# The last block's expert gathers in two token halves, the first half's second network beside block 2's

## The chip, the cores and the metric

One NeuronCore of a Trainium2 chip runs the whole program. The metric is device time in microseconds (us) of one execution, lower is better. TensorE (PE) multiplies matrices, VectorE (DVE) and ScalarE (ACT) work element by element, GpSimd (POOL) issues the gathers, SyncE (SP) issues the other transfers, and 16 DMA engines carry both.

## The reference, cut to what matters

Two networks run one after the other on 512 tokens of 1024 numbers, in float32.

```python
h = h + token_mix(rmsnorm(h, w), ...)            # attention and a gated recurrence
h = h[:, N_META:]
h = h + peer_ffn(rmsnorm(h, ffn_w), ...)         # expert layer
x = rmsnorm(h, final_norm_w)                     # end of the first network
...
# peer_ffn, per token: 8 heads choose 16 experts each, by the top 16 of two lists of keys
u = u_table[experts]                             # 128 rows of 1024 numbers
hid = gelu(einsum('nkd,nd->nk', u, xb)) * gates
y = einsum('nk,nkd->nd', hid, v_table[experts])
...
# second network
q, k, v, z_a, u_b, v_b, z_b, g_a, g_b = split(rmsnorm_2(x, g) @ w_in)
y_a = stick_breaking_attention(q, k, v) * silu(z_a)   # 8 heads of 64, causal
y_b = spatial_gating(gelu(u_b), gelu(v_b), ...) * silu(z_b)
merged = sigmoid(g_a) * (y_a @ w_up_a) + sigmoid(g_b) * (y_b @ w_up_b)
x = x + merged @ w_out
return rmsnorm_2(x, final_norm_g)
```

`spatial_gating` mixes the 128 tokens of a chunk through a masked matrix: a token of the first 64 sees only the first 64, so a half of 64 tokens can be computed once it and what stands before it are there.

## The kernel before, in words

**Blocks and gathers.** The 512 tokens are four blocks of 128 (0 to 3). The expert layer of a block takes 128 gathers (`SLOTS`); each fetches 128 rows of 8 KB (u and v of one expert side by side), 1 MB, into one of 8 places of a ring (`RING`). All 512 gathers are one queue of POOL. A gather serves 64 tokens with two experts each; even gathers serve the first 64 tokens of the block and odd ones the second 64. Two gathers make one **tick**, so the program has 256 ticks, 64 to a block. In a tick DVE forms the dot products with u (L2046), ACT applies the gelu, DVE spreads the results into a 128x64 matrix per gather (L2055, L2056), and PE adds the v rows to the block's sums `psum_y` (`weighted_rows`; matmuls named py). Only then is the ring place free for the next gather.

**The rest beside it.** Everything else (the first network of later blocks, the key scores, the second network of earlier blocks) is put between the ticks by `make_plan`, a list `PLAN` that all engines follow in its order. The second network runs for the groups `POST = [(0, 1), (2,), (3,)]`. For each group its weights pass by once, as 60 tiles of 512 KB (SP, L816): 28 for q, k, v and the gates (`q2 k2 v2 za ub vb zb`), 16 for `ga gb`, 8 for `ua ud`, 8 for `wo`. There are 4 places for tiles (`NW`); at the end 7 more in the ring (`XW`). Group (0, 1) stands in ticks 128 to 206 and group (2,) ticks 207 to 255.

**The end.** When the last gather's sums are there, block 3 has its whole second network left: `hu` takes the sums, norms and turns them, then 60 tiles follow, with the 8 heads' stick-breaking attention between them (`zp` scores, `zl` logarithms, `zd` on DVE, `ze`, `zt` transposes, `zv` values), and at the end `ya`, `yo`, `ua`, `mh`, `wo`, `fl`. The first load of this stretch waits until the last gather has landed.

**Choosing.** `top_part` finds a head's 16 experts in 6 parts, one per tick, a head each 8 ticks, two heads ahead of the gathers. It is DVE work.

**Banks.** PE writes into three PSUM banks pa (emptied by ACT) and three pb (emptied by DVE), taken in turn, and two for `psum_y`.

Of the kernel before, what the change touches and what calls it, by code (L numbers as in the profile page):

```python
# [21 lines left out]
W = 512  # L22
HA, DH = 4, 64
# [30 lines left out]
POST = [(0, 1), (2,), (3,)]  # L54
# [10 lines left out]

def heads_per_unit(b):
    return max(1, 4 // (b + 1)) if b != 2 else 1
# [8 lines left out]
def units2(g):  # L76
    return [(b, u) for b in g for u in range(H2 // heads_per_unit(b))]
# [132 lines left out]
def second_rows(g):  # L210


    n = 2 // len(g)
    rows = shared(tiles("q2", g) + tiles("k2", g), 7 // n)
    for name in ("v2", "vb", "ub", "zb"):
        rows += pairs_of(tiles(name, g), n)
    for k, b in enumerate(g):
        rows[-3 + k - len(g) + 1].append(("ln", b))
        rows[-2 + k - len(g) + 1].append(("l2", b))
    gate = pairs_of(tiles("za", g), n)  # L220
# [14 lines left out]
    for c in range(2):  # L235
        up = pairs_of(tiles("ga", g, c), n) + [[("ua", g, c, i) for i in range(2)]]
        if len(g) == 1 and c == 0:
            rows[-1] = rows[-1] + up.pop(0)
        rows += up
        rows += pairs_of(tiles("gb", g, c), n) + [[("ud", g, c, i) for i in range(2)]]  # L240
    wo = tiles("wo", g, 0) + tiles("wo", g, 1)
    if g != POST[0]:
        return rows + [[("mt", b) for b in g]] + pairs_of(wo, n)
    b = g[-1] + 1
    rows += [[("mt", k) for k in g] + [("ldnorm",)]]
    wo = shared(wo, 6)
    for i, name in enumerate(("n1", "m1", "n2")):
        wo[2 + i] = wo[2 + i] + [(name, b)]
    return rows + wo + [[("fin", k) for k in g], [("fd", g[0])], [("fd", k) for k in g[1:]] + [("store", k) for k in g] + [("n3", b)]]


def last_rows(b):
# [6 lines left out]
    fill += [[("ud", g, 0, i) for i in range(2)], [("ud", g, 1, 0)], [("ud", g, 1, 1)]]  # L259
    between = {0: ("hx", b), 2: ("ln", b), 3: ("l2", b), 4: ("sg", b), 5: ("yb", b)}  # L260
    n_units = H2
    for n in range(n_units + 3):
        row = {4: [("fin", b - 1)], 5: [("fd", b - 1), ("store", b - 1)]}.get(n, [])
        for lag, names in ((3, ("zv",)), (2, ("zt",)), (1, ("zd", "ze"))):
            if 0 <= n - lag < n_units:
# [3 lines left out]
        if n < n_units:  # L269
            row += [("zp", b, n // 2)] * (n % 2 == 0) + [("zl", b, n)]  # L270
        rows.append(row + fill[n])
# [6 lines left out]
def use(s):  # L278
# [16 lines left out]
    if name in ("ua", "ud"):  # L295
# [5 lines left out]
            "xt": (0, 2, 0), "s1": (1, 0, 1), "n3": (0, 2, 0), "zs": (0, 1, 0), "zp": (0, 2, 0), "zt": (1, 0, 0), "zv": (1, 0, 0),  # L301
            "sg": (0, 1, 0), "yt": (2, 0, 0), "yb": (1, 0, 0), "yo": (1, 0, 0), "mt": (2, 0, 0), "mh": (1, 0, 0),
            "hu": (0, 2, 0), "qt": (1, 0, 0), "kt": (1, 0, 0)}.get(name, (0, 0, 0))
# [95 lines left out]

def make_plan():  # L400
# [13 lines left out]
    spread(second_rows((2,)), 3 * PER_BLOCK + 15, n, ticks)  # L414
    place_keys(ticks)
    out = []
    for k in range(n):
        b = k // PER_BLOCK
        out += [("dots", k), ("gelu", k)]
        if k % PER_BLOCK == 0 and b:  # L420
            out.append(("take", b - 1))
        g = k // PER_HEAD + LEAD
        if g < HEADS and k % PER_HEAD < 6:
            out.append(("tk", g // HP, g % HP, k % PER_HEAD))
        out += [("mix", k), *ticks[k], ("rows", k)]
    return first + out + [("ldlast",)] + flat(last_rows(NB - 1))
# [3 lines left out]
SUMS_AT = {(s[0][0], s[1]): n + 1 for n, s in enumerate(s for s in PLAN if s[0] in ("r1", "a1"))}  # L430
MIXED_AT = {(s[0][0], s[1]): n + 1 for n, s in enumerate(s for s in PLAN if s[0] in ("r2", "a2"))}
# [42 lines left out]


def stick_bank(b, u):

    return B_AT[("zp", b, u // 2)] - 1 + u % 2 if b == NB - 1 else B_AT[("zs", b, u)]
# [40 lines left out]
def build(nc, t, out):  # L519

    ctx = ExitStack()
    with ctx:
# [3 lines left out]
        def sem(name):  # L526
# [16 lines left out]
        sc = cut(sb("sc", 2 * W)[:, :], 2, W)  # L543
        xnT = cut(sb("xnT", KT * P)[:, :], KT, P)
        qp = cut(sb("qp", 4 * P)[:, :], 4, P)
        fw = sb("fw", D)[:, :]
        tk = Arena(sb("tk", 992 + 2 * BATCH * TOK), 0, 992 + 2 * BATCH * TOK)
        small = Arena(sb("small", 1193), 0, 1193)
# [16 lines left out]
        ss = small.take(22)  # L565
        rs = small.take(21)
# [11 lines left out]
        bs = small.take(NG)  # L578
        iota = small.take(TOP)
# [4 lines left out]
        last_ss = small.take(4)  # L584
        last_tot = small.take(2)
        last_ln, last_half, last_r1, last_r1s, last_ln2, last_s, last_s8 = (small.take(1) for _ in range(7))
# [95 lines left out]
        sga = cut(q2_words, GM2, W)  # L682
        sgb = za
# [4 lines left out]
        ub_last, zb_last, vc_last, vq_last, up_last = (p4.take(W) for _ in range(5))  # L688
        ga_last, gb_last = cut(p4.take(2 * W), 2, W), cut(p4.take(2 * W), 2, W)
        yT_last, merged_last = p4.take(KT * P), p4.take(D)  # L690
        q_rows, k_rows = p4.take(W), p4.take(W)
# [31 lines left out]
        half_ready, hw_ready, y1_read = sem("half_ready"), sem("hw_ready"), sem("y1_read")  # L723

# [6 lines left out]
                  ("normg2", normg2), ("ffnwT", ffnwT), ("bs", bs))  # L731
        LOADED_F, LOADED_C = 16 * len(FIRST), 16 * len(CONSTS)
        POST_CONSTS = 4
        SCORES_READ = {("k2", POST[1]): HEADS - HP + 2, ("v2", POST[1]): HEADS - HP + 4,
                       ("k2", POST[2]): HEADS - HP + 6, ("v2", POST[2]): HEADS}
# [10 lines left out]
        def index2(b):  # L746
            return b - POST_OF[b][0]
# [23 lines left out]

        def key_inputs(b):

            return xn2T[:, :, P * (b - 2):P * (b - 1)] if b >= 2 else xnT
# [9 lines left out]
        def gather_y(b):  # L784

            return SLOTS * (b + 1)

        def norm_weights(b, last):
# [3 lines left out]
            if b == NB - 1:  # L792
                return uv_rows[:, (GATHERS - RING) % RING, 0:D], ld_l, 16
# [3 lines left out]
        def _(sp):  # L797
# [50 lines left out]

            def load_residual(b):
                sp.dma_start(h1[:, b, :], t["x"][P * b:P * (b + 1), :]).then_inc(ld_h, 16)  # L850

            for s in PLAN:
# [23 lines left out]
                elif s[0] == "store":  # L876
                    b = s[1]
                    sp.wait_ge(fin_ready, b + 1)
                    sp.dma_start(out[P * b:P * (b + 1), :], h1[:, b, :]).then_inc(stored, 16)
                elif s[0] == "fl":  # L880
                    for c in (1, 0):
                        half = slice(W * c, W * (c + 1))
                        sp.wait_ge(*((fin_ready, NB) if c else (half_ready, 1)))
                        sp.dma_start(out[P * s[1]:P * (s[1] + 1), half], h1[:, s[1], half]).then_inc(stored, 16)
# [6 lines left out]
            sp.wait_ge(stored, 16 * (NB + 1))  # L891

        @block.tensor
        def _(pe):
# [32 lines left out]

            def rows_tile(src, g, i, n_tiles, bank, full, k0=0):
# [5 lines left out]
                for j, ps in enumerate(open_banks):  # L934
                    for k in range(2):
                        last = mm(ps[:, :], src[:, k0 + 2 * i + k, P * j:P * (j + 1)], w[:, k, :],
                                  i + k == 0, i == n_tiles - 1 and k == 1)
# [7 lines left out]
            def halves_tile(src, c, i, halves):  # L945
# [5 lines left out]
                for k in range(2):  # L951
                    last = mm(halves[c][:, :], src[:, 2 * i + k, :], w[:, k, :], i + k == 0, i == 3 and k == 1)
# [4 lines left out]
            def quarter_transposes(src):  # L957

                ps = a_bank()
                for k in range(4):  # L960
                    last = nc.tensor.transpose(ps[:, P * k:P * (k + 1)], src[:, P * k:P * (k + 1)], ident)
                last.then_inc(a_full, 1)
# [171 lines left out]
            def weighted_rows(k):  # L1134
                b = k // PER_BLOCK
                first, final = k % PER_BLOCK == 0, (k + 1) % PER_BLOCK == 0
                if first:
# [3 lines left out]
                    for c in range(2):  # L1141
                        mm(psum_y[c][:, :], ident, h1[:, b, W * c:W * (c + 1)], True, False)
                pe.wait_ge(mix_ready, k + 1)
                for lo in range(0, BATCH, TG):
# [8 lines left out]
            def stick_scores(b, u):  # L1153
                nh, nk = heads_per_unit(b), P * (b + 1)
                g = POST_OF[b]
                q = cut(q2_words[:, 0:4 * P * len(g)], 4, P * len(g))
                if u == 0 and b == g[0]:
                    pe.wait_ge(a_free, A_AT[("k2", g, 3)])
                ps = b_bank()
                for m, hh in enumerate(unit_heads(b, u)):  # L1160
                    r = slice(DH2 * (hh % 2), DH2 * (hh % 2 + 1))
                    mm(ps[:, nk * m:nk * (m + 1)], q[r, hh // 2, P * index2(b):P * (index2(b) + 1)], k2T[r, hh // 2, 0:nk],
                       True, False)
                    last = mm(ps[:, nk * (m + 1) - P:nk * (m + 1)], ident, stri, False, True)
                last.then_inc(b_full, 1)

            def paired_scores(b, pair):
                q = cut(q2_words[:, 0:4 * P], 4, P)
                if pair == 0:
                    pe.wait_ge(a_free, A_AT[("kt", b)])  # L1170
                banks = [b_bank(), b_bank()]
                for part, ps in enumerate(banks):
                    r = slice(DH2 * part, DH2 * (part + 1))
                    mm(ps[:, :], q[r, pair, :], k2T[r, pair, :], True, False)
                for ps in banks:
                    mm(ps[:, W - P:], ident, stri, False, True).then_inc(b_full, 1)
# [1226 lines left out]
```

## Time and profile before

| | |
|---|---|
| median of 3 runs | 1957.14 us (1956.62 to 1957.34) |
| the profiled execution | 1955.42 us, span 1953.6 us |
| PE, DVE, ACT, POOL busy | 84%, 68%, 34%, 31% of the span |
| mean granted TensorE clock | 0.934 |
| transfers | 729 MB, mean 373 GB/s |

The span is the time from the first to the last instruction; the execution's own time is 1.8 us more. A profile row for a matmul counts records: a float32 matmul is two records, so a weight tile used by one block of 128 tokens (2 matmuls of 512 columns) is 4 records.

### The profile page before, as it was taken

What the parts mean: (1) busy time and instruction counts of PE and PEld (TensorE: products, weight loads), DVE (VectorE), ACT (ScalarE), POOL (GpSimd) and SP (SyncE); (2) the same over time, 40 slices, a digit from 0 to 9 for tenths busy, and PEclk for the clock granted to TensorE, in tenths of its full rate; (3) what the DMA queues carried; (4) which work ended last, traced back from release to release, by engine and by line L of the source; (5) the groups of instructions that cost most, each with busy time, mean ns of one, the idle gap of its engine ahead of it and who ended that gap; (6) DMA issues with size and microseconds to landing.
All of it is one profiled execution on the core that took longest, in us unless ns stands there. A gap on an engine that the chain in (4) does not pass through costs nothing.

```text
span 1953.6 us, 19684 instructions
## 1 busy us (share of the span) xinstructions
PE 1634.3 (84%) x6534; PEld 799.7 (41%) x6534; DVE 1328.8 (68%) x3466; ACT 656.3 (34%) x1224; POOL 600.0 (31%) x529
## 2 busy tenths in 40 slices
PE   7987897779889976888589999789986877877998
PEld 7555553235455443244145434333333322322453
DVE  4356877875788797875876577976665569744242
ACT  3222424242343254222231233521221246311472
POOL 1002333432333343334433333343323325422000
PEclk9997998889999998889899999899998988899999
DMA  7559999999999998999999999999999999999863
GB/s 223 179 169 416 417 417 419 408 417 418 386 413 354 355 416 326 380 419 415 422 413 418 418 414 374 362 400 418 419 417 350 418 419 401 421 418 412 326 235 109
DMA packets 128836, 729.03 MB, mean 373 GB/s; under 512 B 14688, under 2 KB 15856, under 8 KB 63200
## 3 DMA queue, kind: packets, MB, share of 16 engines
q0 software_dynamic: 74272, 537.82, 67.5%
q1 hardware_dynamic: 54464, 189.97, 25.5%
q8 instruction: 52, 0.85, 0.2%
q14 instruction: 48, 0.39, 0.1%
HBM read 725.63 MB, written 2.10 MB: 373 GB/s over the span
## 4 chain that ended last, share of the span: by engine, by line
PE 47%; DMA 23%; DVE 18%; ACT 5%; issue 5%; POOL 1%; POOLq 0%; DVEq 0%; SPq 0%; ACTq 0%
PE pa L919 26%; DMA uv_rows<-in_peer_uv,small 14%; PE py L919 13%; DMA wbuf<-in_wt 8%; PE pb L919 7%; DVE uv_rows L2046 6%; ACT area L1371 2%; ACT L1365 2%; POOL uv_rows L2291 1%; DVE tk L2056 1%; DVE area L2144 1%; DVE tk L2055 1%; DVE small L2033 1%; ACT small L1371 1%; DVE small L1951 0%
## 5 line engine op out<-in xcount | busy, mean ns | idle before, releaser
L2291 POOL DMA_INDIRECT uv_rows<-in_peer_uv,small x512 | 592.2, 1157 | 1182.3 <-PE py L919 967.2
L2046 DVE CUSTOM_DVE_ANT_0 uv_rows<-uv_rows,xrep 128x1024 f32<-128x1024 f32 x512 | 615.7, 1223 | 223.5 <-DMA uv_rows<-in_peer_uv,small 220.6
L919 PE MATMUL py<-uv_rows,tk 128*64 128x512 f32 x2048 | 560.8, 674 | 211.8 <-DVE tk L2056 208.1
L919 PE MATMUL pa<-wbuf,area 128*128 128x512 f32 (+2 forms) x784 | 342.0, 587 | 27.4 <-DMA wbuf<-in_wt 26.7
L1371 ACT ACTIVATE small<-small 128x2 f32<-128x2 f32 (+4 forms) x327 | 70.6, 217 | 849.9 <-DVE small L2046 816.2
L919 PEld LDWEIGHTS py<-uv_rows,tk 128*64 128x64 f32 x2048 | 135.7, 148 | 514.6 <-DVE tk L2056 278.3
L1365 ACT ACT_TABLE_LOAD x250 | 320.8, 1283 | 5.4 <-DVE small L2177 1.0
L919 PE MATMUL pa<-area,wbuf 128*128 128x256 f32 (+2 forms) x1280 | 233.7, 341 | 17.5 <-issue 12.0
L919 PEld LDWEIGHTS pa<-area,wbuf 128*128 128x128 f32 x1280 | 201.3, 199 | 70.6 <-issue 44.5
L919 PEld LDWEIGHTS pa<-wbuf,area 128*128 128x128 f32 (+1 forms) x784 | 134.2, 189 | 229.5 <-issue 176.5
L1371 ACT ACTIVATE area<-pa 128x512 f32<-128x512 f32 (+7 forms) x225 | 89.2, 413 | 267.3 <-PE pa L919 238.0
L919 PE MATMUL pb<-wbuf,area 128*128 128x512 f32 x304 | 142.3, 612 | 11.1 <-DMA wbuf<-in_wt 7.3
L2055 DVE TENSOR_TENSOR tk<-small 128x2 f32<-128x2 f32 x256 | 41.7, 163 | 104.5 <-issue 51.7
L919 PEld LDWEIGHTS pb<-wbuf,area 128*128 128x128 f32 x304 | 55.8, 193 | 97.3 <-issue 81.7
L2056 DVE TENSOR_TENSOR tk<-small,tk 128x128 f32<-128x128 f32 x256 | 74.8, 292 | 8.9
L919 PE MATMUL pa<-area 128*128 128x64 f32 (+7 forms) x392 | 67.7, 345 | 13.7 <-ACT area L1371 12.3
L1371 ACT ACTIVATE area<-area 128x512 f32<-128x512 f32 (+3 forms) x104 | 67.6, 657 | 33.1 <-DVE area L1842 22.7
L919 PE MATMUL pb<-area 128*128 128x128 f32 (+7 forms) x434 | 73.9, 321 | 1.6 <-ACT area L1371 0.9
L919 PEld LDWEIGHTS pa<-area 128*128 128x128 f32 (+2 forms) x392 | 51.2, 207 | 45.3 <-issue 35.3
L919 PEld LDWEIGHTS pa<-xnT,wbuf 128*128 128x128 f32 x512 | 60.2, 194 | 20.0 <-issue 16.4
L919 PE MATMUL pa<-xnT,wbuf 128*128 128x128 f32 x512 | 64.6, 282 | 2.0 <-DVE xnT L1800 1.1
L919 PEld LDWEIGHTS pb<-area 128*128 128x128 f32 (+2 forms) x434 | 53.9, 192 | 18.7 <-issue 12.6
(253 smaller groups left out, 1178.0 us busy)
## 6 DMA issues: line engine op xcount, KB each, us to landing
wbuf<-in_wt SPq DMA_DIRECT2D x300, 512.0 KB
uv_rows<-in_wt SPq DMA_DIRECT2D x36, 512.0 KB, 6.6
uv_rows<-in_peer_uv,small POOLq DMA_INDIRECT x512
wbuf<-in_skT SPq DMA_DIRECT2D x11, 256.0 KB
h<-in_x SPq DMA_DIRECT2D x4, 512.0 KB
an<-in_x SPq DMA_DIRECT2D x3, 512.0 KB
out<-h SPq DMA_DIRECT2D x3, 512.0 KB, 8.3
area<-in_finw SPq DMA_DIRECT2D x2, 512.0 KB, 10.1
```

What stands on the lines that cost most here:

```text
L919: return nc.tensor.matmul(o, l, r, start=start, stop=stop, skip_group_check=True)
L1365: nc.scalar.preload_act_table_set(TABLES[func])
L1371: return nc.scalar.activation(dst, src, func, **more)
L2033: V.tensor_scalar(gate[to, cols], gexps[tok, g % 2, s_::TG], gsum[tok, g % 2, 1:2], None, ALU.mult)
L2046: last = V.tensor_tensor_reduce(uv_rows[:, n % RING, 0:D], uv_rows[:, n % RING, 0:D], xrep[:, b % 2, n % TG, :], 1.0, 0.0, ALU.mult, ALU.a ...
L2055: step(V.tensor_tensor(wcol[:, k % 2, :], dots[:, at:at + BATCH], gate[:, col:col + BATCH], ALU.mult))
L2056: V.tensor_tensor(mix_w[k % 2], token_mask.unsqueeze(1).broadcast_to([P, BATCH, TOK]), wcol[:, k % 2, :].unsqueeze(2).broadcast_to([P, BAT ...
L2144: step(V.tensor_tensor_scan(rcs[:, 0:wide][:, ::-1], seg2[:, 0:wide], soft[:, 0:wide][:, ::-1], 0.0, ALU.mult, ALU.add))
L2291: nc.gpsimd.indirect_dma_start(uv_rows[:, n % RING, :], None, t["peer_uv"], bass.IndirectOffsetOnAxis(ap=expert_ids[:, c:c + 1].bitcast(U3 ...
```

## The change

The gathers of block 3 are put in the order of its halves: 64 for its first 64 tokens (ticks 192 to 223), then 64 for the second. The halves are blocks of their own, 4 and 5 in the code (`HALVES`), here called **half a** and **half b**. The second network's groups become (0, 1), (2, half a) and (half b).

Group (2, half a) again has 49 ticks, 207 to 255, but its order is written out row by row in `late_rows`: block 2's own q, k, v tiles in rows 0 to 5, its attention (a head each two rows) from row 6; half a's sums are taken in row 17 (tick 224); its own q, k, v tiles in rows 18 to 23; the 40 tiles of gates and up projections for both from row 24 to 43, two a row; `wo` in rows 45 to 48. So 12 tiles more are loaded, and each shared tile is multiplied for 128 and for 64 tokens. Half a's attention is 4 units of two heads, with scores at rows 24, 26, 28, 30.

A tile for 64 tokens is multiplied by `product`: the 512 columns are cut in two halves of 256, which go to the lower and the upper 64 partitions of one bank. The end (`last_rows`) is the same network for half b, 60 tiles with 4 units of attention between them, two groups of 4 tiles to a unit. Choosing the experts goes to a head in 6 ticks from tick 142 on (`chosen_part`), so that all heads of block 3 are chosen by tick 214. The final norm and store of block 2 and half a stand in the rows of the end.

```diff
-POST = [(0, 1), (2,), (3,)]
+HALVES = (NB, NB + 1)
+POST = [(0, 1), (2, HALVES[0]), (HALVES[1],)]
...
+LATE = 49
+FIRST_HALF = 17
...
+def late_rows(g):
...
+    at = {(b, u): 6 + 2 * u for u in range(n_units(b))}
+    at.update({(h, u): FIRST_HALF + 7 + 2 * u for u in range(n_units(h))})
...
+    for i, pair in enumerate(pairs_of(tiles("q2", (b,)) + tiles("k2", (b,)) + tiles("v2", (b,)))):
+        put(i, *pair)
+    own = tiles("q2r", (h,)) + tiles("k2r", (h,)) + tiles("v2", (h,))
+    both = [s for name in ("vb", "ub", "zb", "za") for s in tiles(name, g)]
+    for gate, up in (("gb", "ud"), ("ga", "ua")):
+        for c in range(2):
+            both += tiles(gate, g, c) + [(up, g, c, i) for i in range(2)]
+    for i, pair in enumerate(pairs_of(own + both)):
+        put(t + i, *pair)
+    for i, pair in enumerate(pairs_of(tiles("wo", g, 0) + tiles("wo", g, 1))):
+        put(t + 27 + i, *pair)
...
+DENSE = PER_HEAD * 17 + 6
+def chosen_part(k):
+    if k < DENSE:
+        return k // PER_HEAD + LEAD, k % PER_HEAD
+    return 17 + LEAD + 1 + (k - DENSE) // 6, (k - DENSE) % 6
...
-    spread(second_rows((2,)), 3 * PER_BLOCK + 15, n, ticks)
+    for k, row in enumerate(late_rows(POST[1])):
+        ticks[n - LATE + k] += row
...
+            def product(ps, b, rows_, w, start, stop):
+
+                if b not in HALVES:
+                    return mm(ps[:, :], rows_, w, start, stop)
+                for q in range(2):
+                    last = mm(ps[side(q), 0:H], rows_, w[:, H * q:H * (q + 1)], start, stop)
+                return last
...
+                    for i in range(BATCH):
+                        n = BATCH * k + i
+                        for c in range(2):
+                            last = mm(psum_y[c][cell(m, c), :], mix_w[k % 2][:, i, :], uv_rows[:, n % RING, D + W * c:D + W * (c + 1)],
+                                      False, final and i == BATCH - 1)
```

## Rows read from the trace of the kernel before

**Rows 1.** The page: busy shares, the transfers in 40 slices, one group.

```profile
PE 1634.3 (84%) x6534; PEld 799.7 (41%) x6534; DVE 1328.8 (68%) x3466; ACT 656.3 (34%) x1224; POOL 600.0 (31%) x529
...
GB/s 223 179 169 416 417 417 419 408 417 418 386 413 354 355 416 326 380 419 415 422 413 418 418 414 374 362 400 418 419 417 350 418 419 401 421 418 412 326 235 109
...
L2056 DVE TENSOR_TENSOR tk<-small,tk 128x128 f32<-128x128 f32 x256 | 74.8, 292 | 8.9
```

**Rows 2.** The chain that ended last, from 1780 us on: start, us, what.

```profile
1786.45 23.00 DMA uv_rows<-in_peer_uv,small
...
1815.75 14.00 PE pa L919 x32
...
1919.68 0.70 DVE uv_rows L2153
...
1947.88 0.70 DVE h L1977
```

**Rows 3.** The timeline of SP and of PE around the last gather.

```profile
1809.52 1.75 SPq L816 DMA_DIRECT2D wbuf<-in_wt  x4
...
1811.52 1.94 PE L919 MATMUL py<-uv_rows,tk 128*64 128x512 f32 x8 [1.89 <-DVE tk L2056]
```

**Rows 4.** Windows: stretch, length; PE, PEld, DVE, ACT, POOL busy; clock, DMA share, GB/s.

```profile
941.10:981.90 40.80, 21.01 (x74) 5.67 (x72) 34.01 (x92) 9.89 (x19) 19.65 (x17) 0.86 1.01 421
1191.80:1244.10 52.30, 43.81 (x163) 19.91 (x161) 43.00 (x107) 28.55 (x45) 20.69 (x18) 0.84 0.92 352
1244.10:1283.90 39.80, 28.46 (x118) 11.18 (x120) 36.63 (x97) 20.44 (x35) 15.31 (x16) 0.87 0.95 367
...
1490.60:1614.30 123.70, 96.11 (x370) 43.46 (x371) 73.74 (x198) 33.96 (x61) 35.55 (x31) 0.91 1.01 412
1614.30:1694.50 80.20, 59.74 (x226) 22.68 (x225) 74.71 (x198) 44.08 (x79) 37.56 (x33) 0.83 1.00 411
1694.50:1809.40 114.90, 93.12 (x262) 30.98 (x260) 49.61 (x99) 16.72 (x29) 31.95 (x28) 0.97 1.00 408
```

**Rows 5.** The same stretches for line L2046 alone: 4 records are one tick.

```profile
941.10:981.90 40.80, 19.56 (x32) 0.86 1.01 421
...
1490.60:1614.30 123.70, 38.50 (x64) 0.91 1.01 412
```

**Rows 6.** The timeline of PE beside group (0, 1)'s tiles: start, us, instruction.

```profile
1065.56 1.94 PE L919 MATMUL py<-uv_rows,tk 128*64 128x512 f32 x8
1067.43 3.70 PE L919 MATMUL pa<-wbuf,area 128*128 128x512 f32 x8
1071.06 1.94 PE L919 MATMUL py<-uv_rows,tk 128*64 128x512 f32 x8
```

**Rows 7.** The timeline of PE in the end, one attention unit between tiles.

```profile
1853.73 0.60 PE L1182 MATMUL pa<-ident,area 128*128 128x128 f32 x4
1854.26 1.13 PE L919 MATMUL pb<-area 64*128 64x512 f32 x4
1855.32 0.71 PE L919 MATMUL pb<-stri,ident 128*128 128x128 f32 x4
1855.87 3.60 PE L919 MATMUL pa<-uv_rows,area 128*128 128x512 f32 x8
1859.30 3.60 PE L919 MATMUL pa<-wbuf,area 128*128 128x512 f32 x8
1862.73 1.00 PE L919 MATMUL pa<-area 128*128 128x64 f32 x8
```

**Rows 8.** Windows in the end and in two stretches of low clock, columns as in rows 4.

```profile
1820.00:1840.00 20.00, 19.11 (x56) 8.78 (x55) 0.03 (x1) 3.07 (x6) 0.00 (x0) 1.00 1.03 410
...
1815.70:1919.60 103.90, 102.91 (x348) 52.82 (x348) 32.06 (x42) 59.18 (x93) 0.00 (x0) 1.00 0.75 279
...
1480.00:1500.00 20.00, 6.53 (x32) 3.49 (x33) 13.62 (x34) 0.58 (x3) 8.06 (x6) 0.73 0.97 377
...
1600.00:1700.00 100.00, 76.53 (x277) 28.41 (x274) 90.97 (x236) 51.40 (x93) 46.35 (x39) 0.82 1.00 412
```

More of the change, by code:

```diff
@@ L578, in build @@
         bs = small.take(NG)
+        bs_half = cut(small.take(2 * (NG // 2)), 2, NG // 2)
         iota = small.take(TOP)
@@ L955, in halves_tile, with transposed_into, quarters @@
                     open_banks.remove(c)
[L957 to L962, printed above, removed]
+            def transposed_into(ps, parts, full):
+                for k, part in enumerate(parts):
+                    last = nc.tensor.transpose(ps[:, P * k:P * (k + 1)], part, ident)
+                last.then_inc(full, 1)
+            def quarters(src):
+                n = src.shape[1] // P
+                return [src[:, P * k:P * (k + 1)] for k in range(n)]
             def first_rows(name, i):
@@ L1593, in _, with take_quarter_columns @@
+            def take_quarter_columns(dst, ps, end=True):
+                for i in range(2):
+                    last = fn(dst[:, i::2, :], cut(ps[:, P * i:P * (i + 1)], 2, TOK), ACT.Copy)
+                if end:
+                    last.then_inc(a_free, 1)
+            weighed, turned_n = 0, 0
             for s in PLAN:
@@ new lines, in half_rows_up @@
+                    V.tensor_tensor(an[r, 0:W], psum_y[c][r, :], weights, ALU.mult).then_inc(u_ready, 1)
+                ps = cut(bank()[:, :], 4, P)
+                for c in range(2):
+                    last = V.tensor_tensor(turned((b,))[:, 4 * c:4 * c + 4, :], ps[:, :, cell(b, c)],
+                                           normg2[:, 4 * c:4 * c + 4].unsqueeze(2).broadcast_to([P, 4, TOK]), ALU.mult)
+                emptied(last)
+                dve.wait_ge(sq_done, m + 1)
+                fold(half_tot[:, m, :], half_ss[:, m, :], ss_ready)
@@ L2084, in last_products, with half_out @@
+            def half_out(b):
+                col = 16 + nth(b)
+                dve.wait_ge(rf_done, nth(b))
+                dve.wait_ge(ld_f, 16)
+                for q in range(2):
+                    last = V.scalar_tensor_tensor(x1(b)[side(q), :, :], x1(b)[side(q), :, :], rs[side(q), col:col + 1],
+                                                  cut(fw[side(q), :], 2, 2, H)[:, :, q, :], ALU.mult, ALU.mult)
+                last.then_inc(fin_ready, 1)
             def last_products(b, c):
-                half = slice(W * c, W * (c + 1))
+                col = 16 + nth(b)
```

767 lines of the change are left out of this document (476 added, 291 removed).

## The prediction

> **What bounds the kernel now.** I read the page first, its 40 slices before its shares. From the fourth slice to the 37th the transfers run mostly at 413 to 422 GB/s [rows 1], with dips; only the last three slices fall to 326, 235 and 109. PE's 84% is an average over these two stages. In the first the ring of gathers and the weight tiles fill the DMA engines, and I take 418 GB/s as their rate: a gather of 1.049 MB costs 2.51 us, a tile of 0.524 MB 1.25 us, so a tick without tiles 5.02 us and one with two tiles 7.53 us.
>
> The chain shows the other stage. Its last long DMA piece ends at 1809.45 us, when the last gather has landed; from 1815.75 on it is PE nearly all the way to 1919.6, then a serial part to 1953.6 [rows 2]. The windows say the same: in 1815.7 to 1919.6 PE is busy 102.9 of 103.9 us while the transfers run at 279 GB/s [rows 8]. So the end is PE's: from the last py, over at 1813.5 [rows 3], it takes 140.1 us.
>
> Before that, in ticks 208 to 255, three windows (2 x 64 records of L2046 are 32 ticks) run at 408 to 412 GB/s [rows 4, 5]: the transfers bind there, about 1.5% short of their rate.
>
> **The end, for half b.** 8 records of 512 columns take 3.43 us (1855.87 to 1859.30, [rows 7]), 0.43 each, so a tile for 128 tokens costs 1.72 us and 60 cost 103 of the 140. For 64 tokens a tile is 8 records of 256 columns, written alternately to the lower and upper 64 partitions. The trace has no such record, but the py matmuls alternate the same way: 8 records of 512 columns, period 1.87 us [rows 6], half of 3.43. Two at a time they overlap. A pair of 256 columns then costs 0.215 and the tile 0.86 us. Bounds: 0.86, or 1.72 if the halves did not overlap; the floor per small record does not bind, since 8 records of 64 columns fit into 1.00 us [rows 7]. I take 0.86, because py is the same form but for its length. 60 tiles are 51.6 us. A unit of half b's attention is 4 score records of 448 columns in pairs and 4 short ones (1.4 us with a switch of shape), 4 transposes (0.8 with two switches), 16 records of values (1.7): 3.9 us, and 4 units 15.6. Spatial gating and the remaining transposes add 5. PE has 72 us of work.
>
> The weights need more: 60 tiles at the 410 GB/s of [rows 8] are 76.8 us, and none can be asked for before the last gather lands (the load is issued at 1809.52, [rows 3]). With 1.9 us for 0.8 MB of results stored meanwhile and 1 us until the stream runs, the last tile is there 79.7 us after that landing. Its product takes 0.9, and what stands behind the last product today 5.7 (1947.88 to the end, [rows 2]): 86.3. The chain must also hold: in the last rows of attention few tiles are left to multiply, and transposes, exponentials, values, `ya`, `yo`, `ua`, `mh` follow each other. By the same prices that serial part ends at about the same time; I add 2.7 for the two getting in each other's way. From the landing 89 us, against 144.1 before. Counted from the last py it is 83: 4 less for the same distance as today, and 2 because PE will be the later one there (below) and some tiles are in by then. **The end: 140.1 to 83, -57.**
>
> **Ticks 207 to 255.** Twelve tiles and 0.26 MB of norm weights more are 15.7 us at 418 GB/s. That much is sure as long as transfers bind. But they may not. From row 24 on each tick holds two tiles for block 2 (2 x 1.72) and for half a (2 x 0.86) and its py (1.71): 6.87 us. To this come switches between 128 and 64 columns. The period of a py and 8 records is 5.50 us (1065.56 to 1071.06, [rows 6]) and the work in it 5.14, so two switches cost 0.36. The row goes block 2, half a, block 2, half a, py: four switches, 0.72. PE needs 7.59 us a tick and the transfers 7.53: even. What comes on top has no cover. In ticks 231 to 244 that is half a's attention (15.6), the last value and transpose steps of block 2 (2.4), spatial gating of both (2 x 16 records, 3.6) and `yb`, `yo` (1.4): 23 us. The tiles of both groups hold two of three pa banks for two ticks, and attention steps beside them must wait for ACT; where PE works alone such waits are not hidden: 0 to 12, I take 5. Of the sum 4 is off, since today's stretch has its own 1.5% of waits. So +24, bounds 8 (most of it absorbed by the lead of ring and tiles) and 45 (each attention step waits some 3 us).
>
> Half a's `hu` (DVE on the sums, four transposes, ACT's squares and seven small ones) stands in tick 224, where no tile is due before and few after; the same step costs 4.2 us at the end now (1811.52 to 1815.75, [rows 2, 3]). A tick there is 5.0 to 7.5 us of transfers and the ring holds four ticks: I cost it at nothing, 4 us if the ring were empty. The `ldhalf` load stands on SP ahead of half a's tiles, eleven ticks without tiles earlier; late, it would hold those. Block 2's attention in ticks 213 to 230 is what stands in ticks 224 to 239 today at 411 GB/s with DVE busy 74.7 of 80.2 us [rows 4], now without the choosing of experts on top.
>
> **Choosing faster.** In ticks 120 to 127 DVE is busy 34.0 us, 19.6 of it dots [rows 4, 5] and at least 2.3 mixing (8 x 0.29 of L2056, [rows 1]), so choosing costs at most 12.1 us per head, 1.5 us a tick; in 6 ticks instead of 8 it is 0.5 more from tick 142 to 214. Mostly that is idle time of DVE. In the two windows of ticks 160 to 175 it is not: DVE busy 43.0 of 52.3 and 36.6 of 39.8 us, transfers down to 352 and 367 GB/s [rows 4]. With 4 us more work each, up to 8 us; I take 6, low end 0 (a ring that catches up), high end 10.
>
> **Sum.** 1953.6 + 15.7 + 24 + 6 - 57 = 1942.3 us of span, and 1.8 outside it: 1944. This stands against the profiled 1955.4; the median of the runs is 1.7 higher, so one can read a gain of 11 to 12 us, 0.6%.
>
> **The rivals.** *Transfers go on binding* (chance 0.22): the 24 us of the mixed ticks shrink to 0 to 4, choosing is absorbed: 1953.6 + 15.7 + 4 - 57 + 1.8 = 1918 to 1924. For it: in the three windows of ticks 208 to 255 the transfers run at 408 to 412 GB/s with PE busy 74% to 81% [rows 4]. Against it: 23 us of PE work with no gap to fall into.
>
> *The mixed ticks cost more* (0.14), the one that ends on the other side: each attention step of half a waits for a bank that ACT has not emptied, and PE stands with a group open. The 25 ticks from 231 are 8.9 us each in my sum. At 9.4 the gain is gone; at 9.8 the time is 1966.
>
> *The clock falls in the end* (0.08). PE will wait about 0.4 us for every tile. Granted clock is 1.00 while PE is full, but 0.73 in a window with 6.5 of 20 us busy and 0.82 in one with 76.5 of 100 [rows 8]. At the lower level, 1.2 GHz, a tile costs 1.72 us, over its 1.28 of transfer, and PE binds again. Half the end there adds 36 us of PE work less the 5 of slack: 1975. Against it: a PE that falls behind is full again, and full stretches show 1.00.
> The Trainium skill, page "TensorE: Matmul & The Clock Gate", section "HAM oscillation — how this bites in real kernels", warns of just this: a kernel that waits for a transfer at every step is put back to the slow clock each time. By that rule throughout, PE's work in the end would be 144 us and the time about 2015.
> The rows do not bear that out as far as they go (1.00 in a window with 19.1 of 20 us busy), and the sum keeps the full clock.
>
> *The halves do not overlap* (0.03): each half tile 1.72 us, the end as long as before and 41 us more in the mixed ticks: over 2030.
>
> The remaining 0.53 is my forecast, its own range 1932 to 1955.
>
> **The numbers.** A measurement tells 0.2%, 3.9 us, from no change. Faster (under 1953.2): nearly all of the first rival and of the forecast less its upper edge, 0.71. Same: that edge and the near part of the second, 0.11. Slower 0.18. The range 1918 to 1968 leaves out the non-overlap, most of the clock case and the tips.
>
> **What would show it.** After: 256-column records with 128*64 in pairs 0.215 us apart, or this is wrong at the root. The end: GB/s near 410 for 75 us and a PE that waits for DMA wbuf, clock near 1.00. Ticks 231 to 244: PE full, transfers under 400 GB/s, 9 to 10 us a tick. Ticks 160 to 175: about 0.4 us longer each. The last gather's landing near 1850. Wrong would make it: transfers at 418 in the mixed ticks (time near 1920), long waits of PE for ACT there (over 1955), a clock near 0.5 in the end.

## The result and the profile after

The kernel after the change takes **1969.08 us** (median of 13 runs, 1964.11 to 1973.03), the kernel before beside it 1957.85 (13 runs). The ratio is 1.0053 with a 95% interval of 1.0041 to 1.0065: **0.53% slower**, where 0.6% faster was predicted, and just above the stated range of 1918 to 1968. The profiled execution took 1966.47 us with a span of 1964.5.

The page of after, the rows that answer to [rows 1]:

```profile
PE 1643.0 (84%) x7370; PEld 818.6 (42%) x7370; DVE 1340.6 (68%) x3517; ACT 671.8 (34%) x1282; POOL 596.8 (30%) x530
...
GB/s 228 172 160 418 416 417 418 419 418 417 390 401 348 356 416 328 378 418 418 422 418 419 416 408 356 356 402 418 419 391 333 409 402 404 382 332 393 332 405 225
```

The low slices moved. Before, the last three were low because PE bound the end; now the end has one of 405, and 332 to 393 stand ahead of it, where PE multiplies for block 2 and half a together. The same by stages (windows of after, columns as in [rows 4]; the first two are ticks 160 to 175, the third ticks 224 to 231):

```profile
1198.20:1250.10 51.90, 40.26 (x160) 18.21 (x160) 46.01 (x125) 29.03 (x46) 18.50 (x16) 0.82 0.90 339
1250.10:1290.30 40.20, 29.17 (x118) 12.00 (x116) 38.64 (x106) 18.50 (x32) 17.64 (x16) 0.85 0.94 366
...
1605.00:1659.90 54.90, 38.91 (x209) 17.92 (x209) 32.48 (x69) 29.25 (x59) 17.07 (x16) 0.86 0.96 388
1680.00:1784.00 104.00, 103.35 (x524) 46.34 (x522) 53.30 (x103) 45.52 (x75) 25.42 (x24) 1.00 0.96 353
1784.00:1829.00 45.00, 45.00 (x191) 17.11 (x188) 19.53 (x42) 8.51 (x14) 12.50 (x12) 1.00 1.01 408
1850.00:1870.00 20.00, 17.58 (x78) 6.68 (x76) 9.37 (x22) 3.89 (x9) 0.00 (x0) 0.99 0.61 208
1870.00:1880.00 10.00, 10.00 (x78) 6.15 (x76) 1.55 (x5) 2.95 (x11) 0.00 (x0) 0.84 1.02 411
1870.00:1910.00 40.00, 37.87 (x310) 21.73 (x308) 14.90 (x24) 21.42 (x40) 0.00 (x0) 0.96 1.03 409
1910.00:1920.00 10.00, 9.81 (x102) 6.59 (x100) 3.36 (x6) 7.21 (x13) 0.00 (x0) 1.00 0.95 376
1920.00:1930.00 10.00, 7.26 (x65) 4.75 (x61) 2.27 (x5) 5.79 (x13) 0.00 (x0) 0.89 0.46 160
1930.00:1940.00 10.00, 4.46 (x32) 3.19 (x32) 1.92 (x3) 0.87 (x2) 0.00 (x0) 0.67 0.65 215
```

From 1680 to 1829 PE is idle for less than one microsecond. The end runs at 409 GB/s as it should until 1910; then, with 16 tiles not yet asked for, the transfers fall to 160 and 215 GB/s. That is the first thing to explain. SP's timeline in this stretch and the waits of SP (engine, line, waited for: us, times, longest) in 1830 to 1964 say what happens:

```profile
1905.22 3.12 SPq L994 DMA_DIRECT2D uv_rows<-in_wt  x4
1921.87 0.34 SPq L1073 DMA_DIRECT2D out<-h  x1
1922.26 1.25 SPq L994 DMA_DIRECT2D wbuf<-in_wt  x2
1932.08 1.27 SPq L1038 DMA_DIRECT2D out<-h  x2
1933.39 1.08 SPq L994 DMA_DIRECT2D wbuf<-in_wt  x2
```

```profile
SPq L1073 <- DVE h L2586: 13.5, 1, 13.5
SPq L1038 <- DVE h L2380: 8.6, 1, 8.6
```

SP issues in its written order. It stands 13.5 us at the store of block 2 (line 1073) and 8.6 at the stores of half a (line 1038), and behind them stand the last 16 tile loads, 14 of them behind both. When a store is gone the loads behind it go out one right behind the other (behind the second, two to `wbuf` and seven to the ring from 1933.39 to 1938.39), so their places had been free. PE pays at 1937.62 (its timeline):

```profile
1926.88 3.09 PE L1116 MATMUL pb<-wbuf,uv_rows 128*64 128x256 f32 x16 [2.74 <-ACT uv_rows L1585]
...
1937.62 3.68 PE L1116 MATMUL pb<-wbuf,uv_rows 128*64 128x256 f32 x16 [5.54 <-DMA wbuf<-in_wt]
```

The chain that ended last goes the same way (answers to [rows 2]): DVE's norm of half a, the store, the tile behind it, the product.

```profile
1930.54 0.74 DVE h L2380
...
1932.08 0.62 SPq L1038
...
1933.39 4.18 DMA wbuf<-in_wt
1937.62 3.68 PE pb L1116 x16
```

Counted from 1866.4 us, where the last py ends (to within 0.2 us), the end takes 98.1 us; 83 were predicted, 140.1 it was before [rows 3].

The second thing is tick 224, where half a's `hu` stands. Timelines of PE and of ACT in after:

```profile
1605.84 1.94 PE L1116 MATMUL py<-uv_rows,tk 128*64 128x512 f32 x8
1614.09 1.11 PE L1165 MATMUL pb<-ident,an 128*128 128x128 f32 x4 [6.32 <-DVE an L2349]
...
1616.89 2.00 PE L1116 MATMUL py<-uv_rows,tk 128*64 128x512 f32 x8
```

```profile
1608.52 1.28 ACT L1579 ACT_TABLE_LOAD   x1
1609.81 0.20 ACT L1585 ACTIVATE small<-small 128x2 f32<-128x2 f32 x1
1610.04 1.28 ACT L1579 ACT_TABLE_LOAD   x1
...
1613.34 0.59 ACT L1585 ACTIVATE sc<-py 64x512 f32<-64x512 f32 x1 [1.21 <-DVE an L2349]
```

PE's py of tick 224 starts 11.1 us after that of tick 223, where 5 to 6 are usual without tiles. Its mix weights were there at about 1610.5, but on PE it stands behind `hu`'s transposes, and these wait for DVE's products, which stand behind the tick's dots, the mix and a step of block 2's attention. The mix itself waits for ACT, which loads a table of functions (`ACT_TABLE_LOAD`, 1.28 us) just ahead of the tick's gelu and again behind it for `hu`. Ring rows come free with py, so the gathers stop: 292 GB/s from 1615 to 1620, 247 from 1620 to 1625, 382 from 1625 to 1630. Against 418 that is (126 + 171 + 36) x 5 us = 1.67 MB, 4.0 us.

### The profile page after: what moved, and what is told of

It reads as the page before. It is cut to its first block, busy times and chain, and to the rows that moved or that the text cites. A ratio compares the mean times of both kernels' runs of the same rounds, so it can differ in the third digit from the quotient of the medians.

```text
span 1964.5 us, 21550 instructions
## 1 busy us (share of the span) xinstructions
PE 1643.0 (84%) x7370; PEld 818.6 (42%) x7370; DVE 1340.6 (68%) x3517; ACT 671.8 (34%) x1282; POOL 596.8 (30%) x530
## 2 busy tenths in 40 slices
DMA packets 131085, 735.72 MB, mean 374 GB/s; under 512 B 15008, under 2 KB 16688, under 8 KB 65440
## 4 chain that ended last, share of the span: by engine, by line
PE 44%; DMA 24%; DVE 20%; ACT 5%; issue 5%; POOL 2%; SPq 0%; DVEq 0%; POOLq 0%; ACTq 0%
PE pa L1116 22%; DMA uv_rows<-in_peer_uv,small 18%; PE py L1116 13%; PE pb L1116 9%; DVE uv_rows L2304 7%; DMA wbuf<-in_wt 6%; ACT area L1585 2%; ACT L1579 2%; POOL uv_rows L2602 2%; DVE tk L2315 1%; DVE tk L2314 1%; ACT small L1585 1%; DVE area L2452 1%; DVE tk L2255 0%; DVE tk L2256 0%
## 5 line engine op out<-in xcount | busy, mean ns | idle before, releaser
L1116 PE MATMUL pa<-wbuf,area 128*128 128x512 f32 (+3 forms) x1200 | 372.7, 510 | 20.2 <-DMA wbuf<-in_wt 16.4
L1585 ACT ACTIVATE small<-small 128x2 f32<-128x2 f32 (+5 forms) x338 | 73.1, 218 | 826.6 <-DVE small L2304 785.5
L1116 PEld LDWEIGHTS pa<-wbuf,area 128*128 128x128 f32 (+2 forms) x1200 | 151.5, 168 | 237.2 <-issue 197.5
L1585 ACT ACTIVATE area<-pa 128x512 f32<-128x512 f32 (+8 forms) x240 | 89.1, 395 | 273.6 <-PE pa L1116 250.7
L1116 PE MATMUL pb<-wbuf,area 128*128 128x512 f32 (+1 forms) x400 | 144.5, 544 | 7.7 <-issue 3.9
L1116 PEld LDWEIGHTS pb<-wbuf,area 128*128 128x128 f32 (+1 forms) x400 | 57.9, 175 | 95.7 <-issue 84.0
L1116 PE MATMUL pa<-area 128*64 128x64 f32 (+7 forms) x456 | 70.4, 324 | 13.3 <-ACT area L1585 12.0
L1116 PE MATMUL pb<-area 128*128 128x128 f32 (+10 forms) x466 | 77.4, 324 | 2.2 <-ACT area L1585 1.2
L1585 ACT ACTIVATE area<-area 128x512 f32<-128x512 f32 (+4 forms) x104 | 66.9, 650 | 34.3 <-DVE area L2100 23.7
L1116 PEld LDWEIGHTS pb<-area 128*128 128x128 f32 (+4 forms) x466 | 54.4, 186 | 19.7 <-issue 14.3
```

What stands on the lines that cost most here:

```text
L1116: return nc.tensor.matmul(o, l, r, start=start, stop=stop, skip_group_check=True)
L1585: return nc.scalar.activation(dst, src, func, **more)
```

## The experiments

The ratio is always to the kernel before on the same chip; a difference between two ratios is uncertain by some 0.16% (3 us), up to 0.26% for M. "Tick" numbers are those of the gathers, 0 to 255.

| kernel | median us | ratio [95%] |
|---|---|---|
| after the change | 1969.08 | 1.0053 [1.0041, 1.0065] |
| A: stores last | 1959.14 | 0.9998 [0.9987, 1.0009] |
| B: before, its store last | 1958.96 | 1.0005 [0.9994, 1.0016] |
| C: A, 40 half tiles | 1954.90 | 0.9977 [0.9963, 0.9990] |
| D: hu cut in two | 1961.50 | 1.0013 [1.0003, 1.0023] |
| E: A and D | 1955.41 | 0.9975 [0.9965, 0.9986] |
| F: before, choosing faster | 1962.48 | 1.0017 [1.0005, 1.0029] |
| G: both tiles for block 2, then for half a | 1960.77 | 1.0006 [0.9995, 1.0017] |
| H: tiles in ring places | 1966.40 | 1.0035 [1.0022, 1.0049] |
| I: A and H | 1956.47 | 1.0000 [0.9988, 1.0012] |
| J: A, G, H | 1949.64 | 0.9959 [0.9946, 0.9972] |
| K: A, D, G, H | 1942.75 | 0.9924 [0.9910, 0.9937] |
| L: A, D, G | 1948.93 | 0.9946 [0.9933, 0.9960] |
| M: K, choosing faster from tick 150 | 1942.01 | 0.9916 [0.9894, 0.9938] |
| N: K, choosing faster from tick 158 | 1944.10 | 0.9919 [0.9904, 0.9934] |

**A. Both stores behind the last tile.**

```diff
-    more = {3: [("fin", k)], 4: [("fd", k), ("store", k), ("fin", h)], 5: [("fd", h), ("store", h)]}
+    more = {3: [("fin", k)], 4: [("fd", k), ("fin", h)], 5: [("fd", h)]}
...
-    return rows + [[("fl", b)]]
+    return rows + [[("store", k), ("store", h), ("fl", b)]]
```

> The changed kernel, with the stores of block 2 and of half a moved on SP behind the last weight tile. Theory A (those stores wait for the final norm of their rows and hold the last 15 tiles behind them on SP's queue; the transfers stand nearly idle for 10 us there): PE's wait of 5.5 us for a tile and the slow stretch after it go, 8 to 10 us less than the changed kernel, about 1957 us. Rival (the serial part of the end takes that time whatever the tiles do): 0 to 2 us less.

0.55% or 10.8 us came back, by nothing but the order on SP. SP's timeline shows the loads going on and the stores at once when they are asked for:

```profile
1916.07 5.51 SPq L994 DMA_DIRECT2D uv_rows<-in_wt  x7
1927.23 5.81 SPq L994 DMA_DIRECT2D wbuf<-in_wt  x4
1936.60 0.33 SPq L994 DMA_DIRECT2D uv_rows<-in_wt  x1
1936.97 0.43 SPq L1073 DMA_DIRECT2D out<-h  x1
1937.44 1.84 SPq L1038 DMA_DIRECT2D out<-h  x2
```

The end from the last py (over at 1864.8) is 91.0 us; PE's one wait of 5.5 us for a tile is gone. What PE still waits for tiles there is 1.2 us in all (waits of A from 1864 on: total, times, longest):

```profile
PE pa L1116 <- DMA wbuf<-in_wt: 0.8, 4, 0.2
PE pa L1116 <- DMA uv_rows<-in_wt: 0.4, 2, 0.2
```

**B. The same order in the kernel before, as a control** (`store` of block 2 moved from unit row 5 to the row of `fl`).

> The kernel before with its one store in the end behind the last tile on SP, as a control. It waited 19.6 us on SP there. Theory: PE bound that end, so the tiles held by the store were not missed, and the time is the same within 0.2%, ratio 0.999 to 1.001. Rival: the wait on SP cost there as much as in the changed kernel, and 5 us or more come back, ratio below 0.9975.

Same: 1.0005. Yet the store held SP there even longer (waits of SP in before, 1811 to 1953):

```profile
SPq L879 <- DVE h L2276: 19.6, 1, 19.6
```

The same wait, twice: free where PE binds, 10.8 us where the tiles bind. A and B together show the cause, and that it is the change that made the old order dear. A moved both stores at once, so how the 10.8 us divide between them is not shown.

**C. A, with half of the last 40 tiles' bytes.** The last 40 tiles load only the first 512 of their 1024 columns; the products run as ever, on what stood in the other half.

```diff
+                if n >= TAIL + 20:
+                    slot, src = slot[:, 0:W], src[:, 0:W]
                 sp.dma_start(slot, src).then_inc(w_full[SPOTS[n]], 16)
```

> The changed kernel with stores last, and of the last 40 weight tiles only the first half is loaded (the other half keeps what stood there), so 10.5 MB less, 25.6 us of transfers. Theory: with the stores away the transfers bind the end, and PE's own work there is 72 us as predicted, so the end counted from the last py falls from 93 to some 77 us (72 and the serial rest): 14 to 18 us faster than the kernel with stores last, ratio 0.991 to 0.993. Rival: PE or the chain of attention binds as much as the transfers, and less than 5 us come off.

The rival was right: 0.21% less than A, 4 us, not much more than the uncertainty of such a difference. Windows from the last py to the end, of after, of A and of C, one fence each:

```profile
1866.40:1964.50 98.10, 75.10 (x626) 45.72 (x624) 31.30 (x63) 41.12 (x87) 0.00 (x0) 0.92 0.81 315
```

```profile
1864.80:1955.80 91.00, 73.33 (x626) 44.88 (x624) 31.31 (x63) 41.10 (x87) 0.00 (x0) 0.95 0.87 340
```

```profile
1864.70:1952.40 87.70, 71.39 (x626) 45.26 (x624) 31.29 (x63) 41.07 (x87) 0.00 (x0) 0.94 0.66 233
```

PE's work in the end is 71 to 75 us, as predicted (72). But even with PE waiting for no tile at all the end takes 87.7: PE waits 8.8 us for ACT and DVE, 2.7 of it in one piece for ACT's copy of the turned attention rows (`yo`) ahead of `ua`, and the rest, 7.5, is what stands behind the last product. So two bounds lie within 3.3 us of each other, 87.7 for the chain of attention and copies and 91.0 with all the transfers. Nearly all of those 3.3 are 1.2 us of waits for tiles and 1.9 us more of busy PE; what makes PE busier is open, since the mean clock is no lower (0.95 against 0.94).

**D. Half a's hu cut over two ticks.** DVE's products and ACT's squares stay in tick 224. PE's four transposes, DVE's columns and fold and ACT's seven small ones, with the table load ahead of them, are a new step `hv` in tick 225.

```diff
     put(FIRST_HALF, ("ldhalf",), ("hu", h))
+    put(FIRST_HALF + 1, ("hv", h))
...
-    rows = [[("hu", b)], tiles("q2r", g)
+    rows = [[("hu", b), ("hv", b)], tiles("q2r", g)
```

> The changed kernel with nothing but half a's hu cut in two over ticks 224 and 225. Cut on top of the three other edits it gave 6.9 us. Theory: PE's py of tick 224 stood behind a chain over ACT and DVE, and what it loses there is not made up, because from tick 231 on PE is full and passes every delay on: 5 to 7 us under the changed kernel, near 1963 us, ratio 1.002. Rival: the gain came only together with the shorter mixed ticks, where the transfers are the nearer bound, and here it is 0 to 3.

0.40%, 7.8 us, at the upper edge and beyond. PE's timeline in D: py of tick 224 starts 4.8 us after that of 223, and the transposes wait for nothing.

```profile
1606.51 1.94 PE L1117 MATMUL py<-uv_rows,tk 128*64 128x512 f32 x8
...
1611.27 3.55 PE L1117 MATMUL py<-uv_rows,tk 128*64 128x512 f32 x8 [1.96 <-DVE tk L2322]
...
1615.85 0.60 PE L1166 MATMUL pb<-ident,an 128*128 128x128 f32 x4
```

The transfers stay between 393 and 423 GB/s from 1597 to 1650, and from the py of tick 223 to that of tick 231 it is 57.0 us instead of 63.6. So 6.6 us are lost in eight ticks. Which part of the edit gives how much, the transposes or ACT's table load, was not tested. Six microseconds of stall are not caught up there, because right behind it the tiles of half a need all the transfers (416 to 422 GB/s from 1630 to 1650 in both kernels) and then all of PE.

**E. A and D alone**, the two steps that the prediction had at nothing.

> The changed kernel with the two steps repaired that the prediction had priced at nothing, and no other: both stores of results behind the last tile on SP, and half a's hu cut in two. Theory: these two, 10.8 and 7.8 us by themselves, are what turned the sign; they lie in different stretches, so they add: near 1950 us, ratio 0.996. Rival: some of each is the same slack (the tiles of the end would have been late anyway), and the time is 1955 to 1959, no faster than the kernel before.

0.78%, 15.3 us, of the 18.6 that they make singly: they nearly add, and the 3.3 missing are the size of the uncertainty. In microseconds that is the rival's 1955 to 1959, but the interval of the ratio lies below 1. The kernel is 0.25% faster than before. The sign hung on these two steps; the size did not reach the expected 0.4%.

**F. The kernel before with the faster choosing alone** (`chosen_part` and its use in the plan, as in the diff of the change).

> The kernel before, with only the denser choosing of experts (a head in 6 ticks instead of 8 from tick 142 on). Theory (DVE has no room for it in ticks 160 to 175 and 200 to 207): 5 to 9 us slower than before, most of it by tick 208; some may come back in ticks 224 to 239, where DVE then has less to do. Rival (the 9.5 us that the changed kernel is late at tick 208 come from elsewhere): within 2 us of before.

0.17%, 3.3 us, under the theory's 5 to 9 and over the rival's 2. The place was not the one predicted. Windows of ticks 152 to 159 in before, then in F, and F's ticks 160 to 175:

```profile
1137.70:1191.80 54.10, 50.32 (x177) 21.27 (x176) 45.49 (x113) 18.75 (x30) 18.79 (x16) 0.97 1.01 409
```

```profile
1139.50:1198.20 58.70, 52.93 (x182) 22.44 (x181) 48.98 (x127) 20.47 (x33) 17.82 (x18) 0.97 0.99 395
1198.20:1249.70 51.50, 39.61 (x158) 17.80 (x156) 45.65 (x123) 27.68 (x43) 18.31 (x16) 0.87 0.92 344
1249.70:1290.50 40.80, 30.86 (x116) 12.21 (x116) 39.24 (x108) 19.42 (x34) 16.81 (x16) 0.80 0.95 364
```

Ticks 160 to 175 last 92.3 us against 92.1 [rows 4], with 5 us more of DVE work in them: it went into idle time. Instead 4.6 us are lost in ticks 152 to 159, where PE is busy 93% in before and waits longer for the mix weights (5.8 us instead of 3.8); that the choosing is what delays those weights is argued, not tested, and the rest of the 4.6 is not accounted for. About 3 more are lost in ticks 200 to 207, and some of it all comes back from tick 208 on.

**G. Fewer switches of shape in the mixed ticks.** In `rows_tile`, for group (2, half a), the first tile of a tick is held until the second is there; then both are multiplied for block 2 and both for half a. A tick has one pair of switches instead of two.

```diff
+                    last = part(0, w, i)
+                    if i % 2 == 0:
+                        held[:] = [w]
+                        return
...
+                    part(1, held[0], i - 1).then_inc(w_done, 1)
+                    last = part(1, w, i)
```

> The changed kernel, where of two tiles shared by block 2 and half a both are first multiplied for block 2 and then both for half a, so that a tick has two changes between 128 and 64 columns instead of four. Theory (the mixed ticks are bound by PE, and a pair of changes costs 0.36 us): 24 ticks x 0.36 = 8 us less, about 1958 us, the plain mixed tick 7.2 instead of 7.57 us if the transfers let it. Rival (transfers need 7.53 us a tick there anyway): 1 to 3 us less, from the ticks with attention alone.

0.47%, 9.2 us. A plain tick takes 7.2 us instead of 7.57. PE's timeline in after and in G:

```profile
1785.87 5.93 PE L1116 MATMUL pa<-wbuf,area 128*128 128x512 f32 x24
1791.62 1.89 PE L1116 MATMUL py<-uv_rows,tk 128*64 128x512 f32 x8
1793.44 5.93 PE L1116 MATMUL pa<-wbuf,area 128*128 128x512 f32 x24
```

```profile
1785.32 5.58 PE L1116 MATMUL pa<-wbuf,area 128*128 128x512 f32 x24
1790.73 1.89 PE L1116 MATMUL py<-uv_rows,tk 128*64 128x512 f32 x8
1792.55 5.58 PE L1116 MATMUL pa<-wbuf,area 128*128 128x512 f32 x24
```

That shows that PE bounds these ticks, and prices the switch pair at 0.35 to 0.38 us; 0.36 was read from [rows 6]. The Trainium skill ("TensorEngine Tiling (Array Packing)", section "Key Properties") says that a change of tiling mode drains the engine; it gives no price, and the trace agrees that there is one.

Not all mixed ticks win it. In G's profiled execution the py of tick 231 to that of tick 255 takes 189.3 us instead of 195.2, 5.9 less and not 24 x 0.36: from tick 246 on the transfers bind. That execution was the slowest of G's twelve, and the timed 9.2 is uncertain by 3, so the full sum is neither shown nor excluded.

**H and I. The first seven tiles of the end in ring places**, so that they need not wait for PE to empty `wbuf`; H on the changed kernel, I with the stores last as well.

```diff
-        spot = j if j >= NW else (TAIL + j if n >= TAIL else n) % NW
+        spot = NW + j if n >= TAIL and j < XW else (TAIL + j - XW if n >= TAIL else n) % NW
```

> The changed kernel, where the first seven tiles of the end go to the places in the ring, which are free when the last gather lands, and only then four to the old places, which are held by tiles still being multiplied. Theory (the end is bound by its 60 tiles and the transfers lose some 8 us between the last gather and the last py): 6 to 8 us less, about 1959 us. Rival (the end is a chain of dependent steps): 0 to 2 us less.

> The changed kernel with both stores of results behind the last tile on SP, and the first seven tiles of the end in ring places. Theory: the tiles in ring places gave only 3.5 us by themselves because SP's waiting stores held the later tiles and took back what the early ones had won; with the stores out of the way the tiles in ring places are worth 6 to 8 us, and the time is 10.8 + 6 to 8 under the changed kernel: near 1951 us, ratio to the kernel before 0.996. Rival: with the stores away the end is already bound by the transfers from the last gather on, whose total does not change by asking for seven tiles earlier in it, or by the chain of attention; then the tiles in ring places give 0 to 3 on top and the time is 1955 to 1959.

H gave 0.18%, half of what was expected. I has A's ratio (1.0000 against 0.9998), inside the rival's 1955 to 1959, though in the profiled executions its end was 3.9 us shorter, 87.0 instead of 90.9. The theory that the stores had hidden the gain of H is not borne out by the times.

**J, K and L. Together.**

> Stores behind the last tile, first seven tiles in ring places, and one switch of shape pair less in each mixed tick. Theory, that the three losses lie one behind another: from the changed kernel 10.8 for the stores, 9.2 for the switches and 6 to 8 for the tiles in ring places: near 1941 us, ratio 0.991. Rival: they overlap, since fewer switches turn the mixed ticks to the transfers' bound and bring the last gather earlier only, while the end is then longer by what the transfers of the tiles take: half of the 9.2 is lost again, 1946 to 1950, ratio 0.994 to 0.996.

> As the kernel with all three edits, and half a's hu in tick 224 is cut in two: DVE's products and ACT's squares stay, and PE's transposes, DVE's columns and fold and ACT's seven small ones come one tick later, so that PE's py of tick 224 stands no more behind DVE's products. Theory: the stall of PE there was 6.3 us against some 2.8 in other ticks, and the transfers fell to 247 GB/s in it; 3 to 4 us come back, the time is 3 to 4 under the kernel with three edits. Rival: the ring and the tiles make up for the stall in the ticks behind it, where PE then waits for the transfers anyway: 0 to 1 us.

> The best kernel so far (1942.8 us: stores last, fewer switches, hu cut in two, tiles in ring places) without the tiles in ring places. Theory, after the stores-last pair showed no timed difference by them (3.9 us in the profiled executions): they let seven tiles come before the last products of the mixed ticks, worth up to 4 us, so this is 0 to 4 us slower, 1943 to 1947. Rival: without them the end loses 6 us or more, as was worked out at first: 1949 or above.

J lies 0.41% under I: the switches are worth 8 us there too, so they add, but without the 6 to 8 us of the ring places; its time, 1949.64, is the rival's number and not the theory's 1941, though not by the rival's mechanism. K lies 0.35% under J: `hu` costs 6.9 us here, twice the 3 to 4 expected, and 7.8 by itself (D). L is 0.22% (4.3 us) slower than K, so in this company the tiles in ring places are worth something; in the profiled executions the end from the last py is 88.0 us in K and 91.6 in L. Why they are not in I against A stays open; 0.2% is near the limit of what is told apart. K is 0.76% faster than the kernel before.

**M and N. K with the faster choosing begun later** (`DENSE` and `chosen_part` with 18 and with 19 in place of 17).

> The best kernel so far with the faster choosing begun one head, so eight ticks, later: the busiest ticks for DVE (160 to 175) have three chosen ticks' work less. Theory: choosing faster costs 4.7 us by tick 160 and in ticks 160 to 175 because DVE is short there; begun at tick 150 instead of 142 it costs 0 to 2 less, 1941 to 1943. Rival: heads for half a become late, the gathers of ticks 216 and after wait for them, and it is 2 to 10 us slower.

> As the one before, begun two heads (sixteen ticks) later, at tick 158, the last head four ticks later than in the best kernel. Theory: 0 to 3 us less than the best kernel, unless heads are late. Rival: the last head is chosen after its gathers could have been asked for (ring of four ticks): the transfers stop for some ticks before tick 224, 5 us or more slower.

Both are K within the interval. The cost of choosing is not recovered by beginning it one or two heads later, nor does a time show heads that come too late.

## Why the prediction was wrong

Two steps failed, both costed at nothing or not named at all.

*"The last tile is there 79.7 us after that landing."* The step counted the transfers' bytes and the places, the results "stored meanwhile" as 1.9 us of bytes. It did not walk SP's own queue, where those stores stand ahead of 16 tiles and wait for DVE. The final norms were listed as moved into the rows of the end, and their DMAs were priced as bytes only. In before the same store waited 19.6 us; as PE was the bound, no total of the page spoke of it. Cost: 10.8 us (A), and B shows that it arose with the change. The Trainium skill ("DMA: Bandwidth & Descriptors", section "🔬 Anatomy of one DMA — SWDGE (gpsimd) path") says that a wait on a semaphore happens on the sequencer that issues, before dispatch. It says so in a section on GpSimd's path; SP's idle 13.5 and 8.6 us with loads behind it agree for SP.

*"I cost it at nothing, 4 us if the ring were empty"*, of `hu` in tick 224. The cover named was the ring's four ticks and the absence of tiles. But what `hu` holds is py itself, and py is what frees the ring; the ring's rows protect DVE's dots against late transfers, not the transfers against a late py. Cost: 7.8 us (D), 6.6 in the trace.

Together 15.3 us (E) of the 25 by which the median missed. The other steps:

*The end's chain.* This term was short by 8: 91.0 us in A, where 83 stood. "By the same prices that serial part ends at about the same time" as the last tile makes about 80 us from the last py (86.3 from the landing, less the 6 of that step); with no wait for a tile it is 87.7 (C). PE's work, 72 us, was right. The 8.8 us in which PE waits for ACT and DVE have no term of their own, and the 2.7 added stood for something else, chain and transfers getting in each other's way. What stands behind the last product is 7.5 us and not the 5.7 read from before: half b's columns lie in both halves of the partitions, and the timeline shows copies between them and four stores where there were two; what each costs was not tested. "None can be asked for before the last gather lands" held, but it was not the only gate. The first four tiles go to `wbuf`, whose places come free only as PE works off the mixed ticks, and the seven for the ring stand behind them on SP (SP's timeline in after):

```profile
1854.36 10.83 SPq L994 DMA_DIRECT2D wbuf<-in_wt  x4
1865.23 3.63 SPq L994 DMA_DIRECT2D uv_rows<-in_wt  x7
```

So the transfers run at 208 GB/s in 1850 to 1870, and by the bytes moved from 1854.4 on (1.7 MB) three of the 60 tiles were in when the last py ended. It ends 15 us behind the last gather's packets (1851.4), in before 4.6 us behind them (1808.9 to 1813.5).

*Mixed ticks, +24.* Right in kind, a little high: a plain tick takes 7.57 us (predicted 7.59), PE busy 103.35 of 104 us; ticks 231 to 244 (from the py of tick 230 to that of 244) last 126 us where the terms make 134. The waits for a bank that were put at 5 are not there. That gave 8 back. That PE is the bound is shown by G.

*Choosing, +6.* 3.3 us by time (F), in another place than argued. In the changed kernel the lag by tick 208 is 9.5 us, net of 1.9 by which this execution was late from the start.

*Tiles, +15.7.* The page has 735.72 MB against 729.03, 16.0 us at 418 GB/s. Right.

*Half tiles at 0.86 us.* Right: 32 records, four tiles, take 3.62 us in the end, 0.9 each with the stretch's edges (timeline of after):

```profile
1874.80 3.62 PE L1116 MATMUL pa<-uv_rows,area 128*64 128x256 f32 x32
```

*The clock.* The granted clock was 0.84 in 1870 to 1880, behind waits of 1.6 and 0.9 us for DVE, and 1.00 from 1880 to 1920, where PE works beside the transfers and stands 0.2 us at a time for a tile (six times, from 1897 to 1911). It fell to 0.89 and 0.67 in the two stretches where PE stood 2.7 and 5.5 us. Of the slow records there, the 3.68 us (16 records at the pace of the half tiles take 1.8) stand behind the 5.5 us wait and are part of what the stores cost. The 3.09 stand behind ACT's copy, whose wait is there without the stores too. The clock rival did not come. Nor did the rule of the Trainium skill ("TensorE: Matmul & The Clock Gate", section "HAM oscillation — how this bites in real kernels") in the form weighed ahead, in which a wait at every step was enough: the kernel of that section waits far longer at each step than the 0.2 us here, and short waits did not bring the slow clock.

*The second rival's time,* 1966, is nearly what came, and that is chance: its mechanism is not what happened. From the py of tick 230 to that of tick 255 it is 206.7 us, 8.3 a tick on average where it needed 9.4 to 9.8; single ticks with attention took up to 12.3, but PE was busy in them and stood for no bank.

Adding up for the span: the last py ended at 1866.4 instead of 1859.2 (`hu` +7, choosing +3.5, the execution's late start +1.9, mixed ticks -8; 3 stay open), the end took 15.1 more (stores 7.1 in the traces, chain and late tiles 8).

## What to carry to other kernels

When a change makes an engine that was the bound faster, walk the queue of every engine that feeds it once more, in written order, and ask of each waiting instruction what stands behind it: a wait of 19.6 us on SP that cost nothing became one that cost 10.8. A step costed at nothing needs its cover named in the right direction: a ring of gathered rows covers late transfers, while an operation that holds back the consumer, even one placed where no weights are due, holds back the transfers themselves. Put stores that nothing waits for behind the loads that share their queue, and cut a serial step between engines at the point where PE would wait.

## What was unexpected of the hardware

A stall of 6.3 us of PE lost 4.0 us of transfers in the 15 us that followed it, but 6.6 to 7.8 us of time, since the stages behind it had no slack on transfers or on PE. Removing a switch pair of 0.36 us in each of some 25 ticks gave 9.2 us by time and 5.9 in the profiled execution. There the plain ticks ran at 7.2 us up to tick 245, under the 7.53 worked out for their transfers; then one took 8.8, and ticks 247 to 249 took 7.5, where the transfers bind.
